# Fewer and wider vector operations around a mixer and its norms

## The chip, the cores and the metric

The kernel runs on one core of one Trainium2 chip. The metric is the time of one execution on the device in microseconds (us); lower is better. Before the change the median of three runs was 3890.11 us (3886.8 to 3898.13). One more execution was taken with the hardware profiler, and all rows below come from that one.

The core has five engines that run at the same time, each with its own instruction stream in a fixed order: TensorE (PE, matmuls; PEld is its weight load), VectorE (DVE), ScalarE (ACT), GpSimd (POOL) and SyncE (SP). They wait for each other by semaphores. Here POOL does almost nothing but issue indirect DMAs (gathers of table rows), and SP issues all plain DMAs.

## The reference, cut to what matters

One layer over a prompt of 1024 frames and a sample of 64 frames (D = 1024). What the change touches is the first norm, the recurrent group, the rotation and softmax of the attention, and the two norms after them:

```python
def _layer_norm(x, g, b):                      # ln_in, ln1 and ln2
    mu = mean(x); xc = x - mu; var = mean(xc * xc)
    return xc * rsqrt(var + LN_EPS) * g + b

def layer(h):                                  # h = _layer_norm(x, ln_in_g, ln_in_b) once before
    proj = h @ w_in
    m = concat(RWKV7_group(proj), DiffAttn_group(proj)) @ w_out
    h = _layer_norm(ALPHA * h + m, ln1_g, ln1_b)
    f = peer(h)      # per token: 8 heads x 16 chosen experts, rows gathered from peer_u and peer_v
    return _layer_norm(ALPHA * h + f, ln2_g, ln2_b)

# RWKV-7, per time step: S = S * w_t - (S kk_t) b_t + v_t k_t ; y = S r_t
#   then y is normalised per head, * lnx_g + lnx_b, + bonus, * g
# Rotation of q and k, first 16 of 64 columns of each map:
#   rot = [x1 * cos - x2 * sin, x2 * cos + x1 * sin]
# Attention, two maps a head: softmax(q1 k1 * DA_SCALE) - lam * softmax(q2 k2 * DA_SCALE), then @ v
```

For each token `peer` needs 128 rows of 4 KB of `peer_u` (dot products with the token) and 128 rows of `peer_v` (a weighted sum). One gather of 128 rows, one for each partition, brings 512 KB.

## The kernel before, in words

Tokens are worked in five **segments**: four of 256 prompt tokens (two tiles of 128) and the sample of 64 (one tile), nine tiles in all, numbered g = 0 to 8.

**Mixing** is the work of one segment up to the choice of experts. It has the steps `embed` (load x, input norm in `layer_norm`, transposes L1082 into `hT`, first projections), then four pairs of `rwkv` + `levels` + `chunks` (two heads of the recurrence) with one `attn` head pair beside them, then `project` (output projection), `norm` (ln1), `query` and `topk` (choice of 16 experts a head, on DVE: L1715 to L1719 and what follows). In `rwkv` the running sum of the decays is made by a scan (L1525); before the change the sum without the present step, `cumx`, was a second operation (L1526). At the end of `chunks` come reciprocal, products and sums of the head norm (L1580 to L1584). In `attn` the rotation is L1599 to L1604, the row maximum of the scores L1615 and its scaling L1616.

**Gathering** is the experts' work of a tile. For tile g, POOL gathers a `u` row set (L757) into one of 11 places of `ring_u`, DVE multiplies and sums it with the token (L1460), 128 times (64 for the sample). When all are done, ACT applies gelu and DVE multiplies by the gates (L1483, `wgt`). Then POOL gathers `v` row sets (L757) into the 8 places of `ring_v` and PE adds them with their weights into `pacc` (L1113). At the end DVE adds the sum to h (L1476) and applies ln2 by `layer_norm`.

**Order.** Every engine runs one list made at build time (`plan`, `spread`). In round g the `u` parts of tile g and the `v` parts of tile g-1 are dealt out between the steps of the mixing of a later segment by fixed shares (`BUDGET`, `cuts`). So the mixing of segment 0 runs alone, rounds 0 and 1 run beside the mixing of segment 1, rounds 2 and 3 beside segment 2, 4 and 5 beside segment 3, 6 and 7 beside the sample, and round 8 and the last `v` parts alone. An engine never skips ahead in its list: when DVE waits for one result, its later `u` parts wait too, and POOL waits when no place of a ring is free. A round closes on DVE with L1476, L1483 and ln2; right behind the close of rounds 1, 3 and 5 the next segment's `embed` stands in the lists of DVE and PE.

`tl.link` lets an engine wait for its own last instruction, `tl.told` signals another engine and waits as well, `tl.next` waits for one more signal of a semaphore. `arena` is one SBUF tensor whose places are shared by tiles with different lives. The names in the rows: `pm` and `pacc` are PSUM, `block_in` holds the constants and the parameters `par` (one column of 128 values each), `hT` the transposed h, `h` the ring `h1` of four tiles.

## Time and profile before

| | us |
|---|---|
| median of 3 runs (lowest, highest) | 3890.11 (3886.8, 3898.13) |
| the profiled execution, time | 3877.63 |
| its span, first to last instruction | 3875.5 |
| DVE busy | 2501.1 (65% of the span) |
| PE busy | 2799.5 (72%) |
| POOL busy | 2365.5 (61%) |
| ACT busy | 660.3 (17%) |
| moved by DMA | 1330.61 MB, mean 343 GB/s |

The profiled execution took 12.5 us less than the median of the three others. A busy share is a mean over stretches with different limits, so the table says little by itself: the rows below cut the span where the limits change. In the view of stretches each row has the stretch, then busy us and number of instructions for PE, PEld, DVE, ACT and POOL, the granted clock of TensorE as a share of full speed, the mean busy share of the 16 DMA engines, and GB/s. In the views of groups a row has line, engine, operation, out<-in with shapes, count, then busy us and mean ns of one, then the engine's idle time just before them and what ended it. In the view of time it has start and duration in us, and in brackets the idle time before it and its releaser.

### The profile page before, as it was taken

Reading aid. Unit: us, or ns where it says so; the run is one execution under the profiler, and the core shown is the slowest. Engines: PE = TensorE matmul, PEld = TensorE weight load, DVE = VectorE, ACT = ScalarE, POOL = GpSimd, SP = SyncE. Lnnn points to the kernel's source line nnn. Section 1 sums busy time; section 2 is a strip of 40 time slices with the busy share of each in tenths; the row PEclk is TensorE's granted clock in tenths of the full one; section 3 lists DMA queues with packets and bytes.
Section 4 is the critical chain, followed back from the end, with each engine's and each line's share of the span. In section 5 each row is a group of like instructions: output and inputs, shape, how many; then the busy total and the mean of one; then the engine's idle time right before and its main releaser. Section 6 shows DMA issues by size and latency. Waiting matters only on the chain.

```text
span 3875.5 us, 49152 instructions
## 1 busy us (share of the span) xinstructions
PE 2799.5 (72%) x18591; PEld 1501.6 (39%) x18591; DVE 2501.1 (65%) x5849; ACT 660.3 (17%) x1879; POOL 2365.5 (61%) x2194
## 2 busy tenths in 40 slices
PE   7987537787947787859568887877566666586677
PEld 5667425555603454446024444553122222231111
DVE  3435989876895677767956667769645565673411
ACT  3331112331101222201012222100111110000000
POOL 0000357777447777775567767756667777667775
PEclk9888768898978998989889998888788878678799
DMA  3114779999979999999899999998999999999998
GB/s 130 54 58 153 258 277 327 341 397 393 371 272 383 376 409 388 403 405 365 328 362 394 389 380 380 402 386 327 349 397 397 409 395 393 392 361 387 409 395 340
DMA packets 372965, 1330.61 MB, mean 343 GB/s; under 512 B 40348, under 2 KB 75576, under 8 KB 361592
## 3 DMA queue, kind: packets, MB, share of 16 engines
q0 software_dynamic: 314576, 1145.45, 76.5%
q1 hardware_dynamic: 58152, 182.02, 12.4%
q8 instruction: 147, 2.41, 0.3%
q14 instruction: 90, 0.74, 0.0%
HBM read 1315.76 MB, written 11.29 MB: 342 GB/s over the span
## 4 chain that ended last, share of the span: by engine, by line
POOL 29%; DMA 15%; PE 10%; issue 9%; DVE 7%; ACT 0%; DVEq 0%; ACTq 0%; POOLq 0%
POOL ring_u L757 15%; POOL ring_v L757 13%; DMA ring_v<-in_peer_v,idx_t 9%; PE pacc L1113 6%; DMA ring_u<-in_peer_u,idx 4%; PE pm L1074 2%; DVE ring_u L1460 1%; DMA ring_u<-in_peer_v,idx_t 1%; PE pm L1088 1%; DVE arena L1716 1%; DVE arena L1717 1%; DVE arena L1719 1%; DVE arena L1718 1%; DVE arena L1715 0%; DMA wts<-in_sets 0%
## 5 line engine op out<-in xcount | busy, mean ns | idle before, releaser
L757 POOL DMA_INDIRECT ring_u<-in_peer_u,idx x1088 | 1200.4, 1103 | 877.6 <-DVE gates L1705 407.7
L1460 DVE CUSTOM_DVE_ANT_0 ring_u<-ring_u,h 128x1024 f32<-128x1024 f32 x1088 | 1298.7, 1225 | 601.8 <-DMA ring_u<-in_peer_u,idx 572.9
L757 POOL DMA_INDIRECT ring_v<-in_peer_v,idx_t x1024 | 1097.5, 1072 | 586.9 <-PE pacc L1113 310.1
L1113 PE MATMUL pacc<-ring_v,spread_w 128*32 128x512 f32 x4096 | 1083.5, 691 | 483.1 <-DMA ring_v<-in_peer_v,idx_t 478.9
L1113 PEld LDWEIGHTS pacc<-ring_v,spread_w 128*32 128x32 f32 x4096 | 175.6, 116 | 1150.2 <-DMA ring_v<-in_peer_v,idx_t 953.6
L1074 PE MATMUL pm<-hT,wts 128*128 128x256 f32 (+2 forms) x2656 | 529.7, 359 | 17.9 <-DMA wts<-in_sets 13.3
L1074 PEld LDWEIGHTS pm<-hT,wts 128*128 128x128 f32 x2656 | 453.1, 204 | 131.4 <-issue 61.6
L1088 PE MATMUL pm<-arena 64*64 64x64 f32 (+1 forms) x6256 | 328.7, 241 | 97.6 <-DVE arena L1543 41.2
L1088 PEld LDWEIGHTS pm<-arena 64*64 64x64 f32 x6256 | 262.5, 144 | 228.7 <-issue 80.2
L1074 PE MATMUL pm<-wts,hT 128*128 128x384 f32 (+1 forms) x576 | 197.3, 497 | 7.0 <-DMA wts<-in_sets 7.0
L1074 PE MATMUL pm<-wts,mixT 128*128 128x128 f32 (+1 forms) x1152 | 145.6, 281 | 11.1 <-DVEq L544 5.0
L1074 PEld LDWEIGHTS pm<-wts,mixT 128*128 128x128 f32 (+1 forms) x1152 | 137.1, 190 | 28.1 <-issue 24.6
L1074 PEld LDWEIGHTS pm<-wts,hT 128*128 128x128 f32 (+1 forms) x576 | 106.6, 187 | 92.1 <-issue 33.1
L1476 DVE SCALAR_TENSOR_TENSOR h<-h,pacc 128x1024 f32<-128x1024 f32 (+1 forms) x9 | 11.0, 1219 | 185.4 <-PE pacc L1113 185.3
L1715 DVE MAX8 arena<-arena 128x8 f32<-128x128 f32 (+3 forms) x216 | 62.1, 288 | 75.3 <-ACT arena L1038 69.5
L1093 PE MATMUL pm<-arena,block_in 128*128 128x256 f32 (+1 forms) x360 | 101.0, 401 | 0.0
L1082 PE MATMUL pm<-block_in,arena 128*128 128x128 f32 (+1 forms) x72 | 15.0, 380 | 116.6 <-DVE arena L1433 116.6
L1113 PE MATMUL pacc<-ring_u,spread_w 128*32 128x512 f32 x256 | 82.6, 624 | 10.7 <-DMA ring_u<-in_peer_v,idx_t 8.5
L1460 DVE DVE_READ_ACCUMULATOR2_ANT dots<- 128x1 f32 x1088 | 89.3, 82 | 0.0
L1614 DVE MEMSET pm<- 64x64 f32 (+1 forms) x48 | 6.2, 130 | 118.0 <-PE pm L1305 117.8
L1082 PE MATMUL pm<-block_in,h 128*128 128x128 f32 (+1 forms) x72 | 16.0, 399 | 87.8 <-DVE h L1433 87.8
L1305 PE MATMUL pm<-arena 64*128 64x512 f32 (+4 forms) x224 | 77.0, 514 | 0.0
(233 smaller groups left out, 2741.1 us busy)
## 6 DMA issues: line engine op xcount, KB each, us to landing
wts<-in_sets SPq DMA_DIRECT2D x82, 1536.0 KB, 9.4
ring_u<-in_peer_u,idx POOLq DMA_INDIRECT x1088, 7.9
ring_v<-in_peer_v,idx_t POOLq DMA_INDIRECT x1024, 7.3
wts<-in_sets SPq DMA_DIRECT2D x11, 1024.0 KB, 17.2
arena<-in_subkeys SPq DMA_DIRECT2D x5, 1024.0 KB, 13.2
arena<-in_x_prompt SPq DMA_DIRECT2D x8, 512.0 KB, 11.0
out<-arena SPq DMA_DIRECT2D x64, 64.0 KB
out<-h POOLq DMA_DIRECT2D x8, 512.0 KB
```

Source lines behind the costliest of these rows:

```text
L757: pool.indirect_dma_start(out=out, out_offset=None, in_=table, in_offset=bass.IndirectOffsetOnAxis(ap=index.bitcast(U32), axis=0)).then_in ...
L1074: x = pe.matmul(out, lhs(k), rhs(k), start=(k == 0), stop=(k == KT - 1 and not more))
L1088: x = pe.matmul(pm[h, bank, col:col + width], lhs[h], rhs[h], start=start, stop=stop, skip_group_check=True)
L1093: pe.matmul(pm[:, bank, 0:w], ident[:, :], old.rearrange("p c n -> p (c n)")[:, 0:w], start=True, stop=False, skip_group_check=True)
L1113: x = pe.matmul(pacc[out, c, :], spread_w[:, blocks % 2, quad, place % EIGHTH, :], row[:, c * 512:(c + 1) * 512], start=(place == 0), stop ...
L1305: x = pe.matmul(pm[0:r, bank, 0:m], qT[hc, sl(s, t)], keysT[hc, n:n + m], start=True, stop=True)
L1460: v.tensor_tensor_reduce(ring_u[:, row, :], ring_u[:, row, :], h1[:, g % 4, :], 1.0, 0.0, ALU.mult, ALU.add, dots[:, slot:slot + 1]).then_ ...
L1715: tl.link(v.max(values[:, 0:8], x))
L1716: tl.link(v.max_index(places[:, 0:8], values[:, 0:8], x))
L1717: tl.link(v.match_replace(work, values[:, 0:8], x, LOW))
L1718: tl.link(v.max(values[:, 8:16], work))
L1719: tl.link(v.max_index(places[:, 8:16], values[:, 8:16], work))
```

## The change

Nothing changes in the plan; what a step issues does.

1. **Input norm.** `layer_norm` of `embed` keeps statistics, square root, reciprocal and the subtraction with scaling (the new `centre` and one `tensor_scalar`). Gain and bias are no longer applied by two passes over 128x1024 on DVE but when the transposed tile leaves PSUM: there the feature is the partition, so ACT applies them as a scale and a bias of one value for each partition, in eight activations of 128x128 a tile instead of two of 128x512. They come as 16 more columns of `block`, and the two broadcast loads of 512 KB a segment on SP's queue go.
2. **ln1 and ln2.** One `tensor_scalar` and two `tensor_tensor` over 128x1024 become two `scalar_tensor_tensor`.
3. **Decay.** `cumx` and its exponential go. `dec_i` gets a leading column of ones for each chunk (a memset of four values a partition), and the exclusive decay is read from it one place earlier.
4. **Head norm.** Three operations of 128x256 become two `scalar_tensor_tensor`.
5. **Rotation.** Four products and two sums of 128x32 a tile become two products of 128x64 a tile and two sums of 128x64 for both tiles together.
6. **Scores.** The scale moves to the copy of q into `qT`, and the maximum is written negated, so the scaling of the maximum (L1616) goes.

`arena` loses two tiles of 256 columns and gets one with four more, so what lies behind moves by up to a few columns. The lists of PE and POOL keep the same rows.

**DVE at the first tile's `embed`.** Statistics, reciprocal, then the passes over 128x1024; before, then after:

```order
L1425 BN_STATS arena<-arena 128x6 x2
L1426 BN_AGGR arena<-arena 128x2
L1428 RECIPROCAL arena<-arena 128x1
L1429 TENSOR_SCALAR arena<-arena 128x1024
L1432 TENSOR_TENSOR arena<-arena 128x1024
L1433 TENSOR_TENSOR arena<-arena 128x1024
L1425 BN_STATS arena<-arena 128x6 x2
```

```order
L1421 BN_STATS arena<-arena 128x6 x2
L1422 BN_AGGR arena<-arena 128x2
L1424 RECIPROCAL arena<-arena 128x1
L1496 TENSOR_SCALAR arena<-arena 128x1024
L1421 BN_STATS arena<-arena 128x6 x2
```

The two `tensor_tensor` passes are gone; PE's transposes of the tile wait for the last of the passes.

**ACT at the same place.** The eviction of the transposes into `hT`, between the square roots of tile 0 and tile 1; before, then after:

```order
L874 ACT_TABLE_LOAD
L874 ACTIVATE arena<-arena,eps_ln 128x1
L877 ACTIVATE hT<-pm 128x4x128 x2
L874 ACTIVATE arena<-arena,eps_ln 128x1
L877 ACTIVATE hT<-pm 128x4x128 x2
```

```order
L869 ACT_TABLE_LOAD
L869 ACTIVATE arena<-arena,eps_ln 128x1
L875 ACTIVATE hT<-pm,block_in 128x128 x8
L869 ACTIVATE arena<-arena,eps_ln 128x1
L875 ACTIVATE hT<-pm,block_in 128x128 x8
```

Each tile has eight evictions instead of two, and they read the parameters.

**DVE behind the products `kr`, `kt`, `bt` in the first pair.** The rotation, then the first masked product (L1551 before, L1553 after), for which PE's next work waits; before (the first tile's L1599 stands just ahead), then after:

```order
L1600 TENSOR_TENSOR arena<-arena,rope 128x32
L1601 TENSOR_TENSOR arena<-arena,rope 128x32
L1602 TENSOR_TENSOR arena<-arena,rope 128x32
L1603 TENSOR_TENSOR arena<-arena 128x4x8
L1604 TENSOR_TENSOR arena<-arena 128x4x8
L1599 TENSOR_TENSOR arena<-arena,rope 128x32
L1600 TENSOR_TENSOR arena<-arena,rope 128x32
L1601 TENSOR_TENSOR arena<-arena,rope 128x32
L1602 TENSOR_TENSOR arena<-arena,rope 128x32
L1603 TENSOR_TENSOR arena<-arena 128x4x8
L1604 TENSOR_TENSOR arena<-arena 128x4x8
L1551 TENSOR_TENSOR arena<-pm,block_in 128x512
```

```order
L1545 TENSOR_TENSOR arena<-arena 128x256
L1598 TENSOR_TENSOR arena<-arena,rope 128x64 x4
L1600 TENSOR_TENSOR arena<-arena 128x8x8
L1601 TENSOR_TENSOR arena<-arena 128x8x8
L1553 TENSOR_TENSOR arena<-pm,block_in 128x512
```

Twelve operations became six, and both tiles are signalled by the last of them.

The diff, cut to its core:

```diff
-cumx = carve(SEG)
-dec_x = carve(SEG)
-early_end = top[0]
+early_end = top[0] = max(top[0], 5 * SEG + 2 * NCH * CH + 3 * NCH * CH + SEG)
...
-dec_i = carve(SEG)
+dec_i = carve(NCH, CH + 1)
...
-for i, name in enumerate(("ln_in_g", "ln_in_b")):
-    sp.dma_start(ln_mix[:, i, :], ins[name].partition_broadcast(P)).then_inc(S["lnm_in"], 16)
...
-act.activation(hT[:, 4 * i:4 * i + 4, sl(s, t)],
-               pm[:, i, :].rearrange("p (k n) -> p k n", n=P)[:, :, 0:s.rows],
-               ACT.Copy).then_inc(S["t_read"], 1)
+if s.n == 0 and t == 0 and i == 0:
+    act.wait_ge(S["const_in"], 32)
+for k in range(4 * i, 4 * i + 4):
+    x = act.activation(hT[:, k, sl(s, t)], pm[:, i, k % 4 * P:k % 4 * P + s.rows], ACT.Identity,
+                       bias=par[:, LNB + k:LNB + k + 1], scale=par[:, LNG + k:LNG + k + 1])
+x.then_inc(S["t_read"], 1)
...
-act.activation(dec_i[:, 0:w], cum[:, 0:w], ACT.Exp, scale=DECAY)
-act.activation(dec_n[:, 0:w], cum[:, 0:w], ACT.Exp, scale=-DECAY)
-act.activation(dec_x[:, 0:w], cumx[:, 0:w], ACT.Exp, scale=DECAY).then_inc(S["exps"], 1)
+act.activation(dec_i[:, 0:s.chunks, 1:CH + 1], cum[:, 0:w].rearrange("p (c t) -> p c t", t=CH), ACT.Exp, scale=DECAY)
+act.activation(dec_n[:, 0:w], cum[:, 0:w], ACT.Exp, scale=-DECAY).then_inc(S["exps"], 1)
...
-act.activation(st, pm[:, 2, 0:HD], ACT.Copy, scale=dec_i[:, c * CH + CH - 1:c * CH + CH]).then_inc(S["st_new"], 1)
+act.activation(st, pm[:, 2, 0:HD], ACT.Copy, scale=dec_i[:, c, CH:CH + 1]).then_inc(S["st_new"], 1)
...
-act.activation(qT[:, sl(s, t)], pm[:, bank, 0:s.rows], ACT.Copy).then_inc(S["qkT_read"], 1)
+act.activation(qT[:, sl(s, t)], pm[:, bank, 0:s.rows], ACT.Copy, scale=DA_SCALE).then_inc(S["qkT_read"], 1)
...
-x = act.activation(probs[0:r, c, 0:nk], score_map(s, t, c), ACT.Exp, bias=negm[0:r, c:c + 1], scale=DA_SCALE,
+x = act.activation(probs[0:r, c, 0:nk], score_map(s, t, c), ACT.Exp, bias=negm[0:r, c:c + 1],
...
-def layer_norm(x, stats, mv, sd, r, gain, said, dev, ready, src=None, landed=False):
-    src = x if src is None else src
+def centre(stats, mv, sd, r, src, said, dev):
-    tl.link(v.tensor_scalar(x, src, mv[0:r, 0:1], sd[0:r], ALU.subtract, ALU.mult))
+def layer_norm(x, stats, mv, sd, r, gain, said, dev, ready, src=None, landed=False):
+    src = x if src is None else src
+    centre(stats, mv, sd, r, src, said, dev)
-    tl.link(v.tensor_tensor(x, x, gain[0:r, 0, :], ALU.mult))
-    tl.told(v.tensor_tensor(x, x, gain[0:r, 1, :], ALU.add), ready)
+    tl.link(v.scalar_tensor_tensor(x, src, mv[0:r, 0:1], gain[0:r, 0, :], ALU.subtract, ALU.mult))
+    tl.told(v.scalar_tensor_tensor(x, x, sd[0:r], gain[0:r, 1, :], ALU.mult, ALU.add), ready)
...
-layer_norm(x_in[0:s.rows, t, :], st1, mv1, sd1, s.rows, ln_mix, S["mv"], S["sd"], S["h_ready"], landed=t == 0)
+x = x_in[0:s.rows, t, :]
+centre(st1, mv1, sd1, s.rows, x, S["mv"], S["sd"])
+tl.told(v.tensor_scalar(x, x, mv1[0:s.rows, 0:1], sd1[0:s.rows], ALU.subtract, ALU.mult), S["h_ready"])
...
-tl.link(v.tensor_tensor_scan(cum[:, 0:w], restart[:, 0:w], lw[:, 0:w], 0.0, ALU.mult, ALU.add))
-tl.told(v.tensor_tensor(cumx[:, 0:w], cum[:, 0:w], lw[:, 0:w], ALU.subtract), S["cum_ready"])
+tl.told(v.tensor_tensor_scan(cum[:, 0:w], restart[:, 0:w], lw[:, 0:w], 0.0, ALU.mult, ALU.add), S["cum_ready"])
+tl.link(v.memset(dec_i[:, :, 0:1], 1.0))
...
-tl.link(v.tensor_tensor(kr[:, 0:s.chunks, 0, :], chunked(kk[:, 0:w]), chunked(dec_x[:, 0:w]), ALU.mult))
-tl.link(v.tensor_tensor(kr[:, 0:s.chunks, 1, :], chunked(R), chunked(dec_i[:, 0:w]), ALU.mult))
+tl.link(v.tensor_tensor(kr[:, 0:s.chunks, 0, :], chunked(kk[:, 0:w]), dec_i[:, 0:s.chunks, 0:CH], ALU.mult))
+tl.link(v.tensor_tensor(kr[:, 0:s.chunks, 1, :], chunked(R), dec_i[:, 0:s.chunks, 1:CH + 1], ALU.mult))
...
-tl.link(v.tensor_tensor(yraw[:, 0:w], yraw[:, 0:w], nrm[:, 0:w], ALU.mult))
-tl.link(v.tensor_scalar(yraw[:, 0:w], yraw[:, 0:w], par[:, LXG + j:LXG + j + 1], par[:, LXB + j:LXB + j + 1], ALU.mult, ALU.add))
-tl.link(v.tensor_tensor(yraw[:, 0:w], yraw[:, 0:w], bonus[:, 0:w], ALU.add))
+tl.link(v.scalar_tensor_tensor(yraw[:, 0:w], yraw[:, 0:w], par[:, LXG + j:LXG + j + 1], nrm[:, 0:w], ALU.mult, ALU.mult))
+tl.link(v.scalar_tensor_tensor(yraw[:, 0:w], yraw[:, 0:w], par[:, LXB + j:LXB + j + 1], bonus[:, 0:w], ALU.add, ALU.add))
...
+r = s.rows
-    r = s.rows
-    x = qk[0:r, t, :].rearrange("p (g d) -> p g d", d=HD)
-    xa, xb = x[:, :, 0:8], x[:, :, 8:16]
-    g = s.first_tile + t
-    cos = rope[0:r, g, None, 0:8].to_broadcast([r, 4, 8])
-    sin = rope[0:r, g, None, 8:16].to_broadcast([r, 4, 8])
-    tl.link(v.tensor_tensor(r1[0:r], xa, cos, ALU.mult))
-    tl.link(v.tensor_tensor(r2[0:r], xb, sin, ALU.mult))
-    tl.link(v.tensor_tensor(r3[0:r], xb, cos, ALU.mult))
-    tl.link(v.tensor_tensor(r4[0:r], xa, sin, ALU.mult))
-    tl.link(v.tensor_tensor(xa, r1[0:r], r2[0:r], ALU.subtract))
-    tl.told(v.tensor_tensor(xb, r3[0:r], r4[0:r], ALU.add), S["roped"])
+    x = qk[0:r, t, :].rearrange("p (g d) -> p g d", d=HD)[:, :, 0:ROT].rearrange("p g (a d) -> p g a d", a=2)
+    for i, out in enumerate((by_cos, by_sin)):
+        factor = rope[0:r, s.first_tile + t, None, None, 8 * i:8 * i + 8].to_broadcast([r, 4, 2, 8])
+        tl.link(v.tensor_tensor(out[0:r, 4 * t:4 * t + 4, :].rearrange("p g (a d) -> p g a d", a=2), x, factor, ALU.mult))
+x, g = qk[0:r, 0:s.tiles, :].rearrange("p t (g d) -> p (t g) d", d=HD), slice(0, 4 * s.tiles)
+tl.link(v.tensor_tensor(x[:, :, 0:8], by_cos[0:r, g, 0:8], by_sin[0:r, g, 8:16], ALU.subtract))
+turn = v.tensor_tensor(x[:, :, 8:16], by_cos[0:r, g, 8:16], by_sin[0:r, g, 0:8], ALU.add)
+turn.then_inc(S["roped"], s.tiles)
+tl.next(S["roped"], s.tiles)
...
-tl.link(v.tensor_reduce(mx[0:r, of], sc, AX.X, ALU.max))
-tl.told(v.tensor_scalar(negm[0:r, of], mx[0:r, of], -DA_SCALE, None, ALU.mult), S["max_ready"])
+tl.told(v.tensor_reduce(negm[0:r, of], sc, AX.X, ALU.max, negate=True), S["max_ready"])
```

## Rows read from the trace of the kernel before

**Rows 1.** Stretches of the span: busy us by engine, granted clock, DMA share, GB/s.

```profile
30.00:330.00 300.00, 260.40 (x2520) 199.04 (x2518) 107.46 (x257) 102.06 (x308) 0.00 (x0) 0.86 0.20 69
...
408.00:717.00 309.00, 177.37 (x1504) 140.93 (x1504) 277.31 (x647) 70.20 (x193) 180.58 (x137) 0.77 0.81 290
...
955.00:1147.00 192.00, 129.31 (x608) 70.78 (x606) 166.59 (x563) 17.12 (x44) 98.99 (x98) 0.87 0.93 354
...
1180.00:1740.00 560.00, 434.02 (x3466) 245.76 (x3465) 383.42 (x718) 122.81 (x339) 420.34 (x385) 0.91 1.01 398
1740.00:1975.00 235.00, 164.95 (x711) 78.10 (x711) 194.10 (x605) 22.86 (x57) 131.86 (x127) 0.85 0.89 338
...
1400.00:1450.00 50.00, 44.16 (x305) 25.43 (x306) 37.73 (x70) 14.07 (x43) 39.33 (x36) 0.97 1.03 410
```

**Rows 2.** In order of time, all engines, the second tile of the first `embed`.

```profile
20.51 1.97 PE L1082 MATMUL pm<-block_in,arena 128*128 128x128 f32 x8 [4.51 <-DVE arena L1433]
```

**Rows 3.** Groups by shape on ACT: evictions from PSUM.

```profile
L877 ACT ACTIVATE hT<-pm 128x512 f32<-128x512 f32 x16 | 9.3, 597 | 39.6 <-PE pm L1082 39.6
...
L974 ACT ACTIVATE arena<-pm 128x128 f32<-128x128 f32 x32 | 9.0, 280 | 114.9 <-PE pm L1286 114.9
```

**Rows 4.** Groups by shape on DVE, the passes over 128x1024.

```profile
L1429 DVE TENSOR_SCALAR h<-pm,arena 128x1024 f32<-128x1024 f32 x8 | 10.8, 1344 | 0.3
L1432 DVE TENSOR_TENSOR arena<-arena 128x1024 f32<-128x1024 f32 x8 | 9.8, 1226 | 0.3
...
L1429 DVE TENSOR_SCALAR h<-h,mv,sd 128x1024 f32<-128x1024 f32 x8 | 6.5, 814 | 0.3
...
L1622 DVE SCALAR_TENSOR_TENSOR arena<-arena 128x1024 f32<-128x1024 f32 x4 | 5.1, 1285 | 0.1
```

**Rows 5.** Groups by shape on DVE, the narrower operations of the pairs.

```profile
L1438 DVE SCALAR_TENSOR_TENSOR arena<-arena,block_in 128x256 f32<-128x256 f32 x48 | 23.3, 485 | 1.7
...
L1448 DVE TENSOR_TENSOR arena<-arena 128x64 f32<-128x64 f32 x64 | 14.6, 229 | 2.2
...
L1526 DVE TENSOR_TENSOR arena<-arena 128x256 f32<-128x256 f32 x16 | 6.8, 426 | 0.5
...
L1599 DVE TENSOR_TENSOR arena<-arena,rope 128x32 f32<-128x32 f32 x32 | 6.3, 197 | 5.6 <-ACT arena L968 4.8
...
L1616 DVE TENSOR_SCALAR arena<-arena 128x1 f32<-128x1 f32 x32 | 4.9, 154 | 1.1
```

**Rows 6.** In order of time, all engines, second pair of segment 0.

```profile
127.54 0.70 PE L1190 MATMUL pm<-arena,block_in 128*128 128x256 f32 x2
...
127.86 0.69 DVE L1551 TENSOR_TENSOR arena<-pm,block_in 128x512 f32<-128x512 f32 x1
...
138.35 0.17 DVE L1616 TENSOR_SCALAR arena<-arena 128x2 f32<-128x2 f32 x1
...
143.43 0.36 ACT L984 ACTIVATE arena<-pm,arena 128x128 f32<-128x128 f32 x1
```

**Rows 7.** Who waited for whom: us in total, times, longest.

```profile
DVE ring_u L1460 <- DMA ring_u<-in_peer_u,idx: 572.9, 195, 18.3
...
PE pm L1082 <- DVE arena L1433: 116.6, 9, 53.7
...
PE pm L1082 <- DVE h L1433: 87.8, 9, 20.3
```

**Rows 8.** In order of time, all engines, the closes of rounds 1 and 3.

```profile
1160.11 1.94 PE L1082 MATMUL pm<-block_in,arena 128*128 128x128 f32 x8 [10.96 <-DVE arena L1433]
...
1165.22 0.99 POOL L757 DMA_INDIRECT ring_v<-in_peer_v,idx_t  x1 [32.48 <-PE pacc L1113]
...
1959.62 1.94 PE L1082 MATMUL pm<-block_in,arena 128*128 128x128 f32 x8 [11.11 <-DVE arena L1433]
...
1964.77 0.96 POOL L757 DMA_INDIRECT ring_v<-in_peer_v,idx_t  x1 [8.98 <-PE pacc L1113]
```

**Rows 9.** One line, POOL's gathers of `u` rows: ns min/median/max.

```profile
L757 POOL DMA_INDIRECT ring_u<-in_peer_u,idx x1088: 933/939/2024, 410.6 to 3699.2; - x182
```

More of the change, by code:

```diff
@@ L60 @@
 EIGHTH = 8
-MU, W0, A0, KKW, KAW, RKW, LXG, LXB, SHIFT, SUBG = 0, 14, 18, 22, 26, 30, 34, 38, 42, 56
-NPAR = 57
+MU, W0, A0, KKW, KAW, RKW, LXG, LXB, SHIFT, SUBG, LNG, LNB = 0, 14, 18, 22, 26, 30, 34, 38, 42, 56, 57, 65
+NPAR = 73
 ROW_A, ROW_B = 4, 12
@@ L465, in build @@
         o_sq = carve(P)
-        r1, r2, r3, r4 = (o_sq[:, 32 * i:32 * i + 32].rearrange("p (a b) -> p a b", b=8) for i in range(4))
         probs = carve(2, SEQ)
+        by_cos, by_sin = (probs[:, 0, 512 * i:512 * i + NT * 4 * ROT].rearrange("p (g d) -> p g d", d=ROT) for i in range(2))
         attT = probs[:, 1, :].rearrange("p (k n) -> p k n", n=P)
-        mx = carve(2)
         negm = carve(2)
@@ L1719, in top16 @@
     tl.link(v.max_index(places[:, 8:16], values[:, 8:16], work))
-_INS = ['x_prompt', 'x_sample', 'ln_in_g', 'ln_in_b', 'rw_w2', 'rw_a2', 'rw_g2', 'ln1_g', 'ln1_b', 'peer_u', 'peer_v',
+_INS = ['x_prompt', 'x_sample', 'rw_w2', 'rw_a2', 'rw_g2', 'ln1_g', 'ln1_b', 'peer_u', 'peer_v',
         'ln2_g', 'ln2_b']
@@ L1770, in parameters @@
 def parameters(inputs):
-    names = ("shift_mu", "rw_w0", "rw_a0", "rw_kk", "rw_ka", "rw_rk", "rw_lnx_g", "rw_lnx_b", "state_shift", "da_subln_g")
+    names = ("shift_mu", "rw_w0", "rw_a0", "rw_kk", "rw_ka", "rw_rk", "rw_lnx_g", "rw_lnx_b", "state_shift", "da_subln_g", "ln_in_g", "ln_in_b")
     cols = [np.asarray(inputs[n]).reshape(-1, P).T for n in names]
```

## The prediction

> **What bounds the kernel now.** I read the view of stretches first, because a mean over the span hides that the limit changes. It shows four kinds of stretch [rows 1].
>
> First, from 30 to 330 us, segment 0's mixing runs alone: PE is busy 260 of 300 us, DVE 107, no gather is under way. PE and DVE hand work to each other here, so a DVE operation counts only where PE waits for it.
>
> Second, DVE holds everything: 408 to 717 us and 955 to 1147. In the one DVE is busy 277 of 309 us in 647 operations; with some 30 ns between two, 12 us of real waits are left. In the other it is 167 of 192 and 563 operations, which leaves 8. The DMA share is 0.81 and 0.93. 1740 to 1975 (194 of 235) is the same for the next segment, and it comes once more before 2770.
>
> Third, 1180 to 1740 us: DVE is busy 383 of 560, but the DMA share is 1.01 and 398 GB/s are moved; the fullest 50 us move 410. The mixing of the other segments beside their rounds looks the same, 717 to 955, 1975 to 2550 and 2770 to 3350 us. Here transfers are the limit. 398 against 410 leaves 3%, some 60 us over these 1950 us, which are lost to waits between engines.
>
> Fourth, the closes of rounds. The view of waits leads there: PE stands 116.6 us before the transposes of the input norm and 87.8 before those of ln1, nine times each, for DVE's last pass [rows 7]. Behind the close of round 1, PE waits 10.96 us for the input norm of the next segment, and POOL, which has stood for 32.48 us, may gather again only when PE has gone on with `v` [rows 8].
>
> **The change part by part.** Durations per operation, from [rows 4, 5], with about 30 ns between two linked operations (L1526: 0.5 us idle for 16).
> - Input norm: two passes of 1.226 us go, 2.5 us a tile with the gaps, nine tiles: 22.6 us.
> - ln1: 1.344 + 2 x 1.226 = 3.80 becomes two of the form that L1622 shows, 2 x 1.285 = 2.57: 1.2 us a tile, 11 in all. ln2: 0.814 + 2.45 = 3.27 to 2.57: 0.7 a tile, 6 in all.
> - Decay: 0.426 + 0.03 goes; the memset of four columns is not in the trace, I take L1616's 0.154 for it: 0.3 a pair.
> - Head norm: 3 x 0.426 to 2 x 0.485, and one gap less: 0.3 a pair.
> - Rotation of two tiles: 12 x 0.197 + 12 gaps = 2.8, to six of 128x64. I take L1448's 0.229: 1.6. That saves 1.2 a pair. The new pattern has runs of eight in four dimensions, which no row shows. From above it is bound by L1526 (four times the columns, 0.426: then 2.7, saving nothing), from below by L1599's 0.197 (saving 1.4). L1448 has just this number of columns and a repeated operand, so I stay with it.
> - Scores: 0.154 + 0.03 for each of 56 maxima, 0.4 to 0.8 a pair of two tiles. I take the negated maximum at the price of the plain one.
>
> So a full pair loses 2.2 to 2.6 us of DVE, and the kernel some 80 of 2501. ACT loses 20 exponentials, and none of them was waited for: in the second pair the exponentials follow the square root that DVE waits for. The two broadcast loads are 5 x 1 MB of 1331 MB; they are issued just ahead of a close, where DMA has room, and I count them at nothing (at 400 GB/s they would be 13 us if all were on the path). No wait is added that can come late: the parameters that ACT waits for are in the block that PE waits for before anything starts.
>
> Now what lies on the path:
> 1. First `embed`. PE waits for the second tile's last pass [rows 2]; DVE works through both tiles without a stop but for the square roots, so 2 x 2.5 = 5.0 come off. Against it, the last bank is now evicted by four activations instead of one of 0.597. A 128x128 copy takes 0.280 [rows 3]: 1.1 us one behind the other, 0.5 more than before; overlapped, 0.2 more. I take 0.4: **4.6**.
> 2. Rotation in segment 0. In the second pair L1551 starts at 127.86, right behind the rotation, and PE's level work waits for what follows L1551. PE's third product L1190 ends at 128.24, and the operation that needs it would stand at 128.2 if all came 1.1 earlier [rows 6]. So 1.0 for each of pairs two to four; in the first pair I take nothing, since PE was still late with its products there. **3.0**. The scaled maximum is hidden here: L1616 ends at 138.5 and ACT takes it at 143.43 [rows 6]. Head norm and decay lie beside PE's projections: nothing.
> 3. ln1 of tile 0, PE waiting: **1.2**.
> 4. 408 to 717: ln1 of tile 1 (1.2), two input norms (5.0), almost two pairs (4.2), 10.4 in all. DVE is not quite alone here (DMA 0.81), so I count 85%: **8.8**.
> 5. ln1 in segments 1 to 3: it stands at the head of the second kind of stretch, and PE waits for it [rows 7]. 3 x 2 x 1.2 = 7.4, at 90%: **6.6**.
> 6. Closes of rounds 1, 3 and 5: ln2 and the first tile's input norm stand between the gates and PE's transposes, 0.7 + 2.5 = 3.2 each [rows 8]. POOL's stall of 8.98 us behind round 3 is longer than 3.2, so it counts whole there too. The second tile's 2.5 us are not on the path: gathers issued after the stall have not landed then. 3 x 3.2 = **9.7**.
> 7. The last ln2 ends the span: 0.7. The sample's ln1: half of 1.2. Together **1.3**.
> 8. Third kind of stretch: ten full pairs at 2.4 and four of the sample at 1.3, 29 us of DVE. What is lost to waits there is 3%; a sixth of the 29 comes back: **5** (floor 0, ceiling 29).
>
> The sum is 4.6 + 3.0 + 1.2 + 8.8 + 6.6 + 9.7 + 1.3 + 5 = 40.2. The profiled execution took 3877.6 (span 3875.5 and 2.1 around it), so it would take 3837. It lay 12.5 below the median of the three runs, so on their scale the time is 3890 - 40 = **3850 us**.
>
> **A rule weighed.** POOL needs 0.939 us for a gather in the median and 2.024 at most [rows 9]. The Trainium skill ("SBUF — State Buffer", section "Who interferes with whom") says that a DVE operation with two SBUF inputs shuts out a GpSimd instruction that reads SBUF, that one in a two-port mode shuts it out entirely, and that whoever comes first holds the port for its whole instruction. By that rule every pass that goes also frees POOL, at most 1.1 us for a gather that it met, and ln2's `tensor_scalar` turns from one kind into the other. POOL stands for DVE in the closes anyway, so this counts between 408 and 717 us alone, where four passes of input norm and one of ln1 go: by the rule the sum would be up to 5 us larger. The spread from 0.939 to 2.024 agrees with it; no row here says which operations cause it. I leave the sum as it is.
>
> **The rivals.**
> - *Gathers take it back.* If transfers already limit 408 to 717 and 955 to 1147 (shares 0.81 and 0.93), DVE's gain turns into waits for `ring_u`. For it: DVE waits 572.9 us for that ring in the whole kernel [rows 7]. Against it: in these two stretches all its waits together are 20 us. Left are terms 1, 2, 3, 7 and two thirds of 6, about 17: 3873.
> - *The pairs count fully.* In the third kind of stretch PE, POOL and DVE also wait for each other, and DVE's share of a pair might be on that chain. For it: the 60 us lost there. Term 8 becomes 29 and term 4 whole: 40 + 24 + 2 = 66, 3824.
> - *The new operations cost more than the rows say.* Rotation at its upper bound takes 3.0 from term 2, 2 from term 4 and 1 from term 8: 3856.
> - *TensorE's clock.* The granted clock is 0.86 from 30 to 330 us, with PE busy 260, and 0.77 from 408 to 717, where PE often stands [rows 1]. If the shorter DVE stretches bring PE's work closer together and the grant falls in the first stretch, PE pays there: at 0.72 it is 260 x (0.86/0.72 - 1) = 51 us, more than the 40 gained: 3900. It decides from 0.745 down. Against it: the clock is highest (0.91, 0.97) where PE is busiest.
>
> **How the numbers follow.** The forecast has 0.56 (3842 to 3860), the gathers 0.20, full pairs 0.12, dearer operations 0.08, the clock 0.04. No change means within 0.3%, 3878 to 3902, about what a measurement of this kernel can tell apart. A clock case of 0.04 is counted as slower. Of the gathers' 0.20, 0.08 lie above 3878. So faster 0.56 + 0.12 + 0.12 + 0.08 = 0.88, same 0.08, slower 0.04. The range leaves out the upper end of the gathers, the clock, and the full pairs beyond half: 3828 to 3874.
>
> **What would show it.** Right: the second `embed` tile's transposes start near 15.4 instead of 20.51; the same transposes behind round 1 follow the gates 3.2 us sooner; DVE busy falls to about 2425; round 0 opens near 401 and closes near 700; the stretches at 1.01 DMA share stay as long as they are within a few us. Wrong: DVE waits for `ring_u` between 408 and 717 by far more than before (the gathers), a rotation of more than 2 us (the new pattern), a granted clock under 0.8 in segment 0's mixing, or stretches of the third kind shorter by 5 us and more each.

## The result, and the profile after

The changed kernel took 3839.5 us in the median of four runs (3831.8 to 3840.6), the kernel before 3888.5 beside it (3883.7 to 3898.1): a ratio of 0.988, interval 0.984 to 0.991. A second set of six runs on another chip gave 3838.0 against 3890.6, ratio 0.987 (0.984 to 0.989). So the change is worth about 50 us. The forecast was 3850, or 40 less than before.

The head of the page of the kernel after; its profiled execution took 3840.6 us:

```profile
span 3838.8 us, 48972 instructions
PE 2818.1 (73%) x18591; PEld 1504.0 (39%) x18591; DVE 2425.7 (63%) x5633; ACT 668.8 (17%) x1913; POOL 2372.1 (62%) x2194
...
DMA packets 371523, 1325.36 MB, mean 345 GB/s; under 512 B 40188, under 2 KB 75416, under 8 KB 360152
```

VectorE's busy time fell from 2501 to 2425.7 us, where 2425 was forecast. 5.2 MB are loaded less.

The forms that took the place of the old passes, groups by shape on DVE and (last line) ACT; busy us, mean ns of one, idle before:

```profile
L1432 DVE SCALAR_TENSOR_TENSOR h<-pm,arena 128x1024 f32<-128x1024 f32 x8 | 10.3, 1284 | 0.3
L1432 DVE SCALAR_TENSOR_TENSOR h<-h,mv,ln 128x1024 f32<-128x1024 f32 x8 | 10.3, 1286 | 0.3
L1496 DVE TENSOR_SCALAR arena<-arena 128x1024 f32<-128x1024 f32 x8 | 6.6, 820 | 0.3
L1598 DVE TENSOR_TENSOR arena<-arena,rope 128x64 f32<-128x64 f32 x64 | 14.3, 224 | 10.2 <-ACT arena L965 8.4
L1601 DVE TENSOR_TENSOR arena<-arena 128x64 f32<-128x64 f32 x16 | 3.9, 243 | 1.7
L1528 DVE MEMSET arena<- 128x4 f32 x20 | 1.2, 62 | 1.4
L875 ACT ACTIVATE hT<-pm,block_in 128x128 f32<-128x128 f32 x64 | 23.2, 468 | 21.8 <-PE pm L1079 21.8
```

The two-operation norms cost what L1622 of [rows 4] showed (1.285). The rotation's new pattern costs 0.224 to 0.243 (the sums of L1600 stand at 0.225) where I took 0.229 from [rows 5], so the upper bound of 0.426 did not come true. The memset takes 0.062 in place of 0.154. Only the eviction on ScalarE was priced from a row that looked alike and wasn't: 0.28 for a plain 128x128 copy in [rows 3], 0.468 here with two parameters per partition, from start to end of one. In the train of eight they overlap and end 0.35 apart.

Below are the waits of the kernel after that answer to [rows 7] (us in total, times, longest):

```profile
DVE ring_u L1460 <- DMA ring_u<-in_peer_u,idx: 600.5, 202, 18.7
...
PE pm L1079 <- DVE arena L1496: 95.4, 7, 51.1
...
PE pm L1079 <- DVE h L1433: 75.4, 9, 18.2
```

TensorE stands 21 us less before the input norm's transposes and 12 us less before those of ln1. VectorE waits 28 us more for its ring (12 more in the second pair of profiles). Some of the 75 us of work that it lost may be waited away where gathers run; no run here separates that from chance. Between the opening and the close of round 0, the stretch that this rival was about, its idle time in front of the row products (L1460) is 14.4 us in both profiles after, for 11.7 and 13.5 before.

The closes of rounds 1 and 3 after, in order of time, PE's transposes and POOL's next gather:

```profile
1137.83 1.94 PE L1079 MATMUL pm<-block_in,arena 128*128 128x128 f32 x8 [7.71 <-DVE arena L1496]
...
1143.59 1.62 POOL L752 DMA_INDIRECT ring_v<-in_peer_v,idx_t  x1 [29.89 <-PE pacc L1110]
...
1939.89 1.94 PE L1079 MATMUL pm<-block_in,arena 128*128 128x128 f32 x8 [7.86 <-DVE arena L1496]
```

Against [rows 8] PE's wait fell from 10.96 to 7.71 and from 11.11 to 7.86: 3.25 us at both, for 3.2 forecast.

The first `embed`: PE's first projection before (its second transposes stand in [rows 2]), then PE and ACT after:

```profile
23.16 7.15 PE L1074 MATMUL pm<-hT,wts 128*128 128x256 f32 x22 [0.69 <-ACT hT L877]
```

```profile
11.75 1.94 PE L1079 MATMUL pm<-block_in,arena 128*128 128x128 f32 x8 [11.75 <-DVE arena L1496]
17.12 1.97 PE L1079 MATMUL pm<-block_in,arena 128*128 128x128 f32 x8 [3.43 <-DVE arena L1496]
21.22 3.36 PE L1071 MATMUL pm<-hT,wts 128*128 128x256 f32 x7 [2.14 <-ACT hT L875]
```

```profile
12.87 2.90 ACT L875 ACTIVATE hT<-pm,block_in 128x128 f32<-128x128 f32 x8 [2.39 <-PE pm L1079]
15.62 0.33 ACT L869 ACTIVATE arena<-arena,eps_ln 128x1 f32<-128x1 f32 x1
18.27 2.90 ACT L875 ACTIVATE hT<-pm,block_in 128x128 f32<-128x128 f32 x8 [2.32 <-PE pm L1079]
```

The second tile's transposes start at 17.12, sooner than the 20.51 of [rows 2] but not at 15.4. ScalarE's list has the eight evictions of the first tile ahead of the square root of the second (15.62), and VectorE waits for that root. Behind the transposes the evictions cost more too: the first projection started 2.65 us after the second transposes before (20.51 to 23.16) and 4.10 after (17.12 to 21.22). Of the 5.0 us taken off VectorE, 1.9 reach PE.

### The profile page after: what moved, and what is told of

Its sections match the earlier page's. It is cut to its first block, busy times and chain, and to the rows that moved or that the text cites. A ratio compares the mean times of both kernels' runs of the same rounds, so it can differ in the third digit from the quotient of the medians.

```text
span 3838.8 us, 48972 instructions
## 1 busy us (share of the span) xinstructions
PE 2818.1 (73%) x18591; PEld 1504.0 (39%) x18591; DVE 2425.7 (63%) x5633; ACT 668.8 (17%) x1913; POOL 2372.1 (62%) x2194
## 4 chain that ended last, share of the span: by engine, by line
POOL 29%; DMA 16%; PE 9%; issue 9%; DVE 6%; ACT 0%; DVEq 0%; ACTq 0%; POOLq 0%
POOL ring_u L752 15%; POOL ring_v L752 14%; DMA ring_v<-in_peer_v,idx_t 10%; PE pacc L1110 5%; DMA ring_u<-in_peer_u,idx 5%; PE pm L1071 1%; DVE ring_u L1460 1%; DMA ring_u<-in_peer_v,idx_t 1%; PE pm L1085 1%; DVE arena L1714 1%; DVE arena L1715 1%; DVE arena L1717 1%; DVE arena L1716 1%; DVE arena L1713 0%; PE pm L1302 0%
## 5 line engine op out<-in xcount | busy, mean ns | idle before, releaser
L1460 DVE CUSTOM_DVE_ANT_0 ring_u<-ring_u,h 128x1024 f32<-128x1024 f32 x1088 | 1299.9, 1225 | 629.5 <-DMA ring_u<-in_peer_u,idx 600.5
L1110 PE MATMUL pacc<-ring_v,spread_w 128*32 128x512 f32 x4096 | 1105.9, 699 | 481.4 <-DMA ring_v<-in_peer_v,idx_t 476.3
L1085 PE MATMUL pm<-arena 64*64 64x64 f32 (+1 forms) x6256 | 330.1, 242 | 82.7 <-DVE arena L1545 36.3
L1460 DVE DVE_READ_ACCUMULATOR2_ANT dots<- 128x1 f32 x1088 | 89.2, 82 | 0.0
L1110 PE MATMUL pacc<-ring_u,spread_w 128*32 128x512 f32 x256 | 81.3, 613 | 10.4 <-DMA ring_u<-in_peer_v,idx_t 8.1
L1316 PE MATMUL pm<-arena 128*128 128x128 f32 (+2 forms) x328 | 59.2, 339 | 22.3 <-ACT arena L992 20.3
```

What stands on the lines that cost most here:

```text
L1085: x = pe.matmul(pm[h, bank, col:col + width], lhs[h], rhs[h], start=start, stop=stop, skip_group_check=True)
L1110: x = pe.matmul(pacc[out, c, :], spread_w[:, blocks % 2, quad, place % EIGHTH, :], row[:, c * 512:(c + 1) * 512], start=(place == 0), stop ...
L1316: x = pe.matmul(pm[0:r, 4, 0:P], attT[0:m, b, 0:r], vals[0:m, b, :], start=(b == 0), stop=(b == nb - 1))
L1460: v.tensor_tensor_reduce(ring_u[:, row, :], ring_u[:, row, :], h1[:, g % 4, :], 1.0, 0.0, ALU.mult, ALU.add, dots[:, slot:slot + 1]).then_ ...
```

## The experiments

Each was run in five rounds. The first four (the three parts and the loads) were on a chip where every kernel took 11% longer: the kernel before 4323.7 us. Segment 0's mixing was as fast there as elsewhere; with gathers under way TensorE and the others stood for their own instructions. This is the page's line of its small products in the first experiment, idle 262.2 us where the kernel before had 97.6 on the first chip, and half of it (135.5) is put down to "issue":

```profile
L1089 PE MATMUL pm<-arena 64*64 64x64 f32 (+1 forms) x6256 | 373.4, 259 | 262.2 <-issue 135.5
```

The ratios of that chip are against its own runs of before. They are coarser, some 15 us to either side.

**The parts one by one.** The edits are shown in short form. First, the input norm alone; its two broadcast loads go with it:

```diff
-    tl.link(v.tensor_tensor(x, x, gain[0:r, 0, :], ALU.mult))
-    tl.told(v.tensor_tensor(x, x, gain[0:r, 1, :], ALU.add), ready)
+    # ACT, at each eviction of 128x128:
+    act.activation(hT[:, k, ...], pm[...], ACT.Identity, bias=par[:, LNB + k], scale=par[:, LNG + k])
```

> The kernel before with the first part alone: the input norm's gain and bias applied by ScalarE at the evictions of the transposes, nothing else. Theory of the prediction, with the first embed as it was now read (1.9 us there, not 4.6): 1.9 + five segments at 0.85 of two passes of 1.23 on each of two tiles where VectorE holds tile 0 of ln1 up (4.2, of which about half reaches the gates) + three closes at 2.5: 12 to 16 us faster, ratio 0.996 to 0.997. Rival 'the gathers take it back': 4 us or less, ratio 0.999 or more. Rival 'VectorE counts fully everywhere' (20 tile passes of 2 x 1.23): 24 us.

4314.8 us, ratio 0.998 (0.995 to 1.001): 9 us faster, with an interval from 22 faster to 5 slower. The 22.6 us of VectorE that go, counted in full, lie at the very edge of it, and it can't tell the forecast's share from nothing.

Second, the two-operation ln1 and ln2 alone:

```diff
-    v.tensor_scalar(x, src, mv, sd, subtract, mult); v.tensor_tensor(x, x, gain, mult); v.tensor_tensor(x, x, bias, add)
+    v.scalar_tensor_tensor(x, src, mv, gain, subtract, mult)
+    v.scalar_tensor_tensor(x, x, sd, bias, mult, add)
```

> The kernel before with the second part alone: ln1 and ln2 in two operations over 128x1024 (subtract and gain, then deviation and bias) in place of three; the input norm keeps its three. Theory of the prediction: 1.2 in segment 0, 6.6 in segments 1 to 3, 1.2 at the stretch 408 to 717, 0.7 at each of three closes, 1.3 at the end: about 12 us faster, ratio 0.997. Rival 'the gathers take it back': 3 to 4 us. Rival 'the new operations cost more' (1.29 to 1.6 us each against 0.81 + 1.23 + 1.23): 8 us at 1.6.

4306.5 us, ratio 0.9947 (0.991 to 0.998): 23 us faster, with an interval of 7 to 38; the 12 expected lie inside it. Since that was the largest surprise, it was measured again on an undisturbed chip:

> The two-operation ln1 and ln2 alone on the kernel before, once more, since the first measurement (ratio 0.9947, 0.9911 to 0.9983) came from a chip on which every kernel took 11% longer with gathers running. Theory of the prediction: 12 us faster, ratio 0.997. Rival 'the surplus of the whole change lies here': 20 us or more faster, ratio 0.995 or less.

3865.3 against 3892.3, ratio 0.992 (0.990 to 0.995). This points to the rival, that the surplus of the whole change lies at least in part here. How much is soft, since the kernel before measured against itself beside it:

> The kernel before against itself, for a second profile of it and for what the measurement tells of no change: ratio 1.000 within 0.3%. If the 8 to 14 us that the profile of after seemed to give back between 1180 and 1665 is of the change, this profile has the head pairs of segment 2 at the same times after the close of round 1 as the first; if it is one execution's chance, they scatter by as much.

3888.6 us in 12 runs, ratio 0.998 (0.996 to 1.000). So these comparisons flatter by up to 0.2%; against these 12 runs the norms are worth 23 us. All VectorE time that they take away is 9 x 1.2 + 9 x 0.7 = 17 us. A gain above that the removed time can't explain; with the flattery taken off, the interval (14 to 32 us) reaches down to it, and the flattery itself is uncertain by as much as its size, so that the forecast's 12 are not safely excluded either. Where the trace is clean it shows exactly the removed time: from 961 to 1164 us, where VectorE holds everything, the kernel with these norms took 199.3 us for 202.4 and 202.3 in the two profiles of before, with 3.1 removed, and PE's wait in the close of round 1 fell by the 0.7 of ln2 and nothing else,

```profile
1156.58 1.94 PE L1082 MATMUL pm<-block_in,arena 128*128 128x128 f32 x8 [10.23 <-DVE arena L1434]
```

and in the second profile of the kernel before it is 10.96 again, to the hundredth:

```profile
1156.69 1.94 PE L1082 MATMUL pm<-block_in,arena 128*128 128x128 f32 x8 [10.96 <-DVE arena L1433]
```

Third, the edits inside the head pairs alone (decay, head norm, rotation, scale and maximum; the first two parts undone):

> The kernel after with its first two parts undone: only the edits inside the head pairs (no exclusive decay sum and exponent, two-operation group norm, the wider rotation, the scale folded into the queries, the negated maximum). Theory of the prediction: 3 in segment 0, 1 in the stretch 408 to 717, 5 for the stretches where the gathers run alongside, and 2 to 3 at the closes: 10 to 12 us faster, ratio 0.997. Rival 'the head pairs count fully' (20 pairs of about 1.5 us of VectorE work each): 30 us, ratio 0.992. Rival 'nothing of them is on the path but segment 0': 3 to 6 us.

4303.5 us, ratio 0.996 (0.993 to 1.000): 16 us faster, nearer to the forecast's 10 to 12 than to the 30 of "the head pairs count fully", which lie at the edge of the interval. The three parts multiply to 0.998 x 0.9947 x 0.9964 = 0.989, against 0.987 and 0.988 for the whole on other chips. Each part is uncertain by 0.003, so this shows no interplay, and would not show one of 20 us.

Fourth, the kernel after with the unused loads put back:

```diff
+    if s.n > 0:
+        for i, name in enumerate(("ln_in_g", "ln_in_b")):
+            sp.dma_start(ln_mix[:, i, :], ins[name].partition_broadcast(P)).then_inc(S["lnm_in"], 16)
...
     # DVE, ahead of the input norm's last pass:
+    if s.n > 0 and t == 0:
+        tl.next(S["lnm_in"], 32)
```

> The kernel after, with the two broadcast loads of the input norm's gain and bias (512 KB each into SBUF) issued again in segments 1 to 4, their data unused. Theory of the prediction (it gave these loads nothing of its own): 0 to 3 us slower than the kernel after, since VectorE finds them landed. Rival 'the stretches with gathers are bound by bytes': 4 x 1.05 MB at about 0.36 MB per us, 8 to 12 us slower than the kernel after, ratio to before 0.990 to 0.991 in place of 0.988.

4283.8 us, ratio 0.993 (0.989 to 0.996). The kernel after itself was not run on this chip. Against the product of the three parts (0.989) the loads would cost 15 us, against nothing the interval also reaches. It is inconclusive, and it leaves the rival open that the loads are part of the gain. The input norm's run bounds them from the other side, since it drops them too. Its gain is at most 22 us, and some 9 of these belong to the norm itself by the clean places (1.9 in the first `embed`, and 2.5 at each of three closes: the whole change took 3.25 off PE's wait there and ln2 alone 0.73, see below). If these 9 carry to the end, the loads are left with 13 us at most, and with nothing by the middle of the interval.

**The kernel after again**, as the base for what follows, on an undisturbed chip:

> The kernel after, unchanged, as the base of the three runs beside it. Prediction: 40 us under the kernel before at 3890, ratio 0.990; measured once 0.988. Rival 'the gathers take it back': 0.996.

3838.0, ratio 0.987 (0.984 to 0.989).

**Where does VectorE's time count?** Two passes over 128x1024 were added to each head pair, first in segments 1 to 4:

```diff
     yield "decay"
+    if s.n > 0:
+        for _ in range(2):
+            tl.link(v.tensor_tensor(probs[:, 0, :], probs[:, 0, :], probs[:, 0, :], ALU.max))
     tl.next(S["nrm_ready"])
```

> The kernel after with two more VectorE passes over 128x1024 (a maximum of a buffer with itself, 1.23 us each by [rows 4]) in each of the 16 head pairs of segments 1 to 4, behind the decay scan: 39 us of VectorE work more. Theory of the prediction (head pairs beside gathers count by about a sixth): 5 to 12 us slower than the kernel after. Rival 'the head pairs count fully': 35 to 40 us slower. Rival 'the gathers take it back': 0 to 3 us slower.

3853.0, ratio 0.991 (0.989 to 0.993): 15 us slower for 39 us of work. And in segment 0, with one memset of the buffer in the first pair:

> The kernel after with the same two passes in each of the four head pairs of segment 0, before any gather runs (4 x 2.45 us and one memset of 128x1024 in the first): 10 us of VectorE work more. Theory of the prediction (TensorE and VectorE alternate there, so it counts in full, and is carried to the end): 8 to 11 us slower than the kernel after, with the opening of the gates 8 to 11 us later. Rival 'what is lost ahead of the gathers is caught up later': gates 8 to 11 us later, the end 0 to 4.

3841.1, ratio 0.987 (0.984 to 0.990): no change. Both of my theories for this one fell: the gates did not open later at all (398.6 us, for 398.3 and 395.9 in the two profiles after). The dose lay in a wait. This is the second pair, DVE in order of time, of the kernel after and then of the dosed one; the two passes run 2.48 us, and the wait for the norm behind them is 1.56 us instead of 4.07:

```profile
117.06 0.29 DVE L1537 TENSOR_SCALAR arena<-arena 128x256 f32<-128x256 f32 x1 [4.07 <-ACT arena L909]
```

```profile
108.73 0.69 DVE L1527 TENSOR_TENSOR_SCAN arena<-block_in,arena 128x256 f32<-128x256 f32 x1 [1.01 <-ACT arena L901]
...
111.01 2.48 DVE L1540 TENSOR_TENSOR arena<-arena 128x1024 f32<-128x1024 f32 x2
115.06 0.29 DVE L1542 TENSOR_SCALAR arena<-arena 128x256 f32<-128x256 f32 x1 [1.56 <-ACT arena L909]
```

So the same dose was put behind the rotation, in front of the masked products (the memset stays where it was):

```diff
     tl.next(S["roped"], s.tiles)
+    if s.n == 0:
+        for _ in range(2):
+            tl.link(v.tensor_tensor(probs[:, 0, :], probs[:, 0, :], probs[:, 0, :], ALU.max))
     yield "rope"
```

> The kernel after with the dose of e_dve_first (two passes of 1.23 us over 128x1024 in each head pair of segment 0, 9.8 us in all) moved from behind the decay scan, where it lay inside a wait of VectorE of 6.3 us, to behind the rotation, in front of the masked products. Theory: the rotation's place is on the alternation of TensorE and VectorE, so the step from the norm to the mask grows from 6.5 to 9.0 us in each pair, the gates open 9 to 10 us later, and the end is 6 to 11 us later than of the kernel after (ratio 0.989 for 0.987). Rival 'what is lost ahead of the gathers is caught up': the same 9.0, the end 0 to 3 us later. Rival 'another wait takes it in': the step from norm to mask grows, but the next one shrinks by as much.

3851.8, ratio 0.989 (0.987 to 0.992): by the ratios 10.5 us over the kernel after, for 9.9 of work. The two were measured on different chips, each ratio is uncertain by 0.0025 (10 us), and the plain times differ by 14; the traces say more. The step from the norm to the mask went from 6.5 to 9.0 us in three of the four pairs, 9.4 in the fourth. The gates opened 15 us later in the profile than in the first of after, the rest of it in TensorE's small products, which scatter so (below). The same 9.9 us cost nothing visible at one place of the pair and lengthened the chain by all of it a few operations further on. DVE in the second pair:

```profile
126.87 0.22 DVE L1602 TENSOR_TENSOR arena<-arena 128x64 f32<-128x64 f32 x1
127.20 0.23 DVE L1603 TENSOR_TENSOR arena<-arena 128x64 f32<-128x64 f32 x1
127.46 2.48 DVE L1608 TENSOR_TENSOR arena<-arena 128x1024 f32<-128x1024 f32 x2
129.98 0.69 DVE L1555 TENSOR_TENSOR arena<-pm,block_in 128x512 f32<-128x512 f32 x1
```

And behind the rotation in segments 1 to 4:

> The same dose behind the rotation in the 16 head pairs of segments 1 to 4, 39 us of VectorE work; e_dve_later, with it behind the scan, was 15 us slower than the kernel after. Theory of the prediction (a sixth counts beside gathers, 85% in the stretch 408 to 717): 4 x 2.45 x 0.85 + 12 x 2.45 / 6 = 8 + 5: 13 us slower. Rival 'the place decides here too' (behind the scan VectorE often has a wait to spare, behind the rotation it has none): 25 to 39 us slower, ratio 0.993 to 0.997.

3854.8, ratio 0.990 (0.988 to 0.993): 14 to 17 us slower, as with the dose behind the scan (15). With gathers under way no effect of the place in the pair shows, within some 13 us. The trace shows why none is to be expected: the wait of 4.07 us in front of the norm exists only in segment 0. In all 16 later pairs of the kernel after, a row product for the gathers (L1460) runs right up to it, with 0.00 us idle, as in the first pair of segment 1:

```profile
560.62 1.22 DVE L1460 CUSTOM_DVE_ANT_0 ring_u<-ring_u,h 128x1024 f32<-128x1024 f32 x1
561.76 0.08 DVE L1460 DVE_READ_ACCUMULATOR2_ANT dots<- 128x1 f32 x1
561.76 0.29 DVE L1537 TENSOR_SCALAR arena<-arena 128x256 f32<-128x256 f32 x1
```

**The order on ScalarE in the first embed**, tested by moving one square root:

```diff
-    for t in range(s.tiles):
-        deviation()                      # the square root of tile t
-        for i in range(2):               # its two halves of evictions
+    for t in range(s.tiles):
+        if s.n > 0 or t == 0: deviation()
+        for i in range(2):
+            if s.n == 0 and t == 0 and i == 1: deviation()
```

> The kernel after with the square root of segment 0's second tile placed on ScalarE between the two halves of the first tile's evictions, since the trace of after shows VectorE waiting 2.75 us for it behind all eight. Theory (the evictions' order ate part of term 1): second tile's transposes about 1.4 us sooner (15.7 for 17.12), the end 1 us or so sooner, ratio as of the kernel after within 0.1%. Rival 'the evictions themselves bound the first embed': transposes sooner, TensorE's next step at 21.2 as before.

```profile
15.54 1.97 PE L1084 MATMUL pm<-block_in,arena 128*128 128x128 f32 x8 [2.04 <-DVE arena L1501]
19.65 2.93 PE L1076 MATMUL pm<-hT,wts 128*128 128x256 f32 x6 [2.14 <-ACT hT L880]
```

The transposes start at 15.54 and the projections at 19.65, both 1.6 us sooner than after; 0.2 of that was there already at the first tile. 3832.3 us, ratio 0.985 (0.983 to 0.988). The trace shows 1.4 us; the rest of the 6 us to the kernel after is within the scatter. PE's step from the second transposes to the first projection stays 4.11 us: that is the evictions' own price, which the order doesn't touch. It is the fastest version measured.

## One profile against another

The first pair of profiles misled me twice before I had a second profile of each. Segment 0's four pairs seemed to gain some 10 us instead of 4, and 1180 to 1665 us seemed to give 10 back. Here are two stretches of the kernel before in its second profile (columns as in [rows 1]). In the first profile [rows 1] they stand with PE busy 260.40 and 434.02 us, at a clock of 0.86 and 0.91:

```profile
30.00:330.00 300.00, 250.49 (x2528) 191.79 (x2526) 112.30 (x263) 102.86 (x311) 0.00 (x0) 0.91 0.21 75
1180.00:1740.00 560.00, 436.48 (x3450) 246.00 (x3449) 382.15 (x714) 121.62 (x335) 422.31 (x382) 0.91 1.01 395
```

The same kernel prepared its first gates 7.4 us sooner in the second profile, at a granted clock of 0.91 for 0.86, and still ended 24 us later. The time from mask to head norm, which is TensorE's chain of small products, was 37.1, 40.6, 38.8 and 38.2 us in the first and 37.1, 37.9, 36.3 and 36.4 in the second; VectorE's own step from the norm to the mask was 7.6 in all eight.

So I took the start times of marked VectorE operations in two profiles of the kernel before, five with the change and no dose where it matters (after twice, the root moved, both doses in segment 0), and the two with doses later. The first marker is the cast (L1666 before) that follows the second tile's choice of experts; every other one is the aggregation of the statistics just ahead of a norm. So an interval that ends at a norm does not hold that norm's own passes; 1164 is the second tile's input norm of segment 2, and 2763 the only one of the sample:

| interval (us in the first profile of before) | before | with the change | difference | forecast |
|---|---|---|---|---|
| 0 to the second tile's gates (487) | 487.4, 480.2 | 476.0, 474.1, 472.6, 476.0 | -9.1 | -9.8 |
| 487 to 961, segment 1's pairs | 474.0, 477.8 | 468.8, 472.0, 468.8, 469.4, 469.2 | -6.3 | -8.6 |
| 961 to 1164, ln1 and close of round 1 | 202.4, 202.3 | 196.7, 196.7, 196.7, 196.7, 196.5 | -5.7 | -5.4 |
| 1164 to 1950, segment 2 and its ln1 | 785.8, 791.3 | 791.7, 783.2, 781.5, 789.6, 786.6 | -2.0 | -3.9 |
| 1950 to 1963, close of round 3 | 13.7, 13.7 | 10.5, 10.5, 10.5, 10.4, 10.5 | -3.2 | -3.2 |
| 1963 to 2550, segment 3's pairs | 586.5, 607.3 | 587.8, 589.5, 591.3, 593.9, 588.6 | -6.7 | -1.6 |
| 2550 to 2763, ln1 and ln2 of the close of round 5 | 213.0, 217.2 | 208.2, 208.4, 208.5, 208.2, 206.7 | -7.1 | -2.9 |
| 2763 to 3528, the sample's input norm, pairs and ln1 | 764.7, 761.5 | 753.4, 751.7, 746.1, 749.3, 751.9 | -12.6 | -4.0 |
| 3528 to the end (of the execution's time), three ln2 | 350.0, 350.4 | 347.7, 347.6, 347.6, 348.6, 347.3 | -2.4 | -0.7 |

(The first row leaves out the dose on the chain. Forecasts are the terms of the sum, shared out over the intervals; they make 40.1, and the differences 55.1.) In the first, second, third and fifth row, where VectorE or its alternation with TensorE holds most of the time, 24.3 us came back for 27.0 forecast; in the other five 30.8 for 13.1. Where VectorE alone sets the time, as from 961 to 1164, one kernel's profiles agree within 0.2 us; where gathers run at full load, within 3 to 21. With the doses later in the kernel, 487 to 961 took 480.0 and 479.8 us: 10.3 more for 9.9 of work. All of it counts there. By the medians, 5 to 7 us are left for the other 29, about a fifth; both dosed profiles were among the slowest of their six runs and show more (21), so a fifth is rather the lower end. The medians are uncertain by several us themselves.

## Why the prediction was right, point by point

The sum of 40 met 49 to 53, inside the range; no rival came true. That it came so near is in part luck: term 1 was too high by 2 us or more, terms 2, 7 and 8 were too low, and the surplus is not explained. By its terms:

1. First `embed`, 4.6: too high. The transposes' gain is 3.4 of the 5.0, since the second root stood behind eight evictions. PE's next step gained only 1.9 (23.16 to 21.22), since the evictions behind the transposes cost 1.45 more, where I had taken 0.4 from a copy without parameters. PE's first operation of segment 0's pairs starts 1.1 us sooner in that profile, 1.8 in one and 2.6 in four others with the change. I had not asked what eight evictions for two do to the list in which the square root stands. e_root_first gave 1.3 back.
2. Rotation, 3.0: right in mechanism, low by one pair. The step from norm to mask is 7.6 us in all four pairs of both profiles of before and 6.5 in all of after: 1.1 each, the first pair included, where I had taken nothing. So 4.4; e_first_chain shows that this place is on the chain: the step grew there by the whole dose.
3. ln1 of tile 0, 1.2: with the 2.6 and 4.4 of terms 1 and 2, and ln1 of tile 1 (1.2, from term 4), it makes 9.4 for the 9.1 measured up to 487.
4. 408 to 717, 8.8, and 5. ln1 in segments 1 to 3, 6.6: the first was a bit high. Round 0 took 307.5 and 309.9 us from its opening to L1483 before, and 301.3 and 302.5 after: 6.8 us less. From 487 to 961, with four pairs and two input norms, 6.3 came back for 8.6, while a dose there costs its full length. The clean row of 961 to 1164 holds one ln1 of two tiles and one close, 5.7 for 2.2 + 3.2.
6. Closes, 9.7: right, 3.25, 3.25 and, for round 5, a wait of 7.81 for 11.04, where the norms alone left 10.32. "POOL stands longer than 3.2, so it counts whole" held.
7. The end, 1.3: low. From 3528 on stand three ln2 of 0.7 each, not one: 2.1, and 2.4 was measured. The sample's ln1 lies in the row above.
8. Third kind of stretch, 5: low. The long mixings came to about 16 in the mean of the profiles (nothing in segment 2 beyond its ln1, 6.7 in segment 3, and 8.9 of the sample's 12.6 when its input norm and ln1 are taken off), with a scatter as large; the doses put a fifth or more of VectorE's time on the path. The surplus of 10 us and more lies from segment 3 on: that a sixth comes back was the mis-sized term. By the prediction's own sign of being wrong, a stretch of this kind shorter by 5 us and more, two of the three speak against it. What makes it is open: the loads that went away (5.2 MB are 13 us at 400 GB/s, if all on the path) or a larger share for VectorE. e_loads_back didn't tell them apart, and it was not measured where it could have; e_input_norm leaves the loads 13 us at most. Against the loads also speaks segment 2, which gained nothing beyond its ln1, though with a scatter of 5 to 10 us.

"Gathers take it back" is out: 17 us were forecast by it, 50 came, although VectorE's ring waits did rise by 12 to 28. "Pairs count fully" is out by e_dve_later and e_late_chain (15 of 39, and at most some 28 by the intervals). "New operations cost more" is out by the rotation's durations; the eviction on ScalarE did cost more, and is in term 1. The granted clock in segment 0's mixing was 0.88, and 0.87 in the second profile; it moves as much between two executions of one kernel.

Of the rule weighed, the Trainium skill's ("SBUF — State Buffer", "Who interferes with whom"), no trace shows a gain: POOL was busy 2372.1 us after, 2365.5 and 2382.1 in the two profiles of before, and 487 to 961 gave less than the sum, not 5 us more. The section also says that the probe behind it saw DMA stalled by `tensor_copy` but not by `tensor_tensor`, which my working left out; the passes of the input norm that it counts are `tensor_tensor`.

## What to carry to other kernels

Price a VectorE operation by its place: in an alternation with TensorE the same 2.5 us lengthened the step in full in front of the product that TensorE waits for, and vanished a few operations sooner, in front of a result of ScalarE that VectorE had to wait for anyway. When work moves to another engine's evictions, read that engine's list, and look at what stands behind them that the first engine waits for. And where gathers run at full load take at least two profiles before a stretch is explained; the stretches that one engine holds can be read from one.

## What the runs showed of the hardware

One chip ran every kernel 11% slower once gathers were under way (the mean rate from 1000 to 2000 us was 315 GB/s in e_input_norm for 367 in the first profile of before), while segment 0, without gathers, took the same time (its gates were ready at 396.1 us in e_loads_back, for 398.3 and 395.9 in the profiles after). Engines stood there for the issue of their own instructions: 148.5 us on one line of PE in 75 waits, up to 18.8 us each, in e_input_norm; 2.2 us in 5 waits in the kernel before.

```profile
PE pm L1089 <- issue: 148.5, 75, 18.8
```

Which other load shared the memory there, if any, no trace tells. A ScalarE eviction of 128x128 with scale and bias from SBUF took 0.468 us from start to end by the profile, against 0.281 for one with a constant scale (L971 after), but in a train they overlap and end 0.35 apart.
